# Experts' input by products with a 0/1 slot matrix instead of a gather; routing per tile inside the output projection; residual gates loaded during attention

## The reference

```
x  = x + gt_a * (attention(...) @ w_o)            # context rows too, in layer 0
h  = rmsnorm(x, g_ffn) * (1 + sc_f) + sh_f        # 512 tokens in layer 0, 256 in layer 1
g  = argmax(h @ w_group + b_group)                # 1 of 4 groups
e1, e2 = top 2 of the group's 8 experts by h @ w_router + b_router
y  = sum over the two of wt_e * (silu(h @ w_gate[e]) * (h @ w_up[e])) @ w_down[e]
x  = x + gt_f * y
```

## Time and profile before

| | us |
|---|---|
| median of 3 runs (2517.99 to 2520.10) | 2518.36 |
| profiled execution | 2517.32 |
| its span | 2515.5 |
| PE busy | 2069.2 (82%) |
| DVE busy | 584.7 (23%) |
| ACT busy | 393.8 (16%) |
| L667, all expert products | 750.1, PE idle before them 197.3 |
| DMA `ring<-in_w_up` in the chain | 28% of the span |

### The profile page before, as it was taken

The page is one execution under the profiler, slowest core; times in us unless marked ns, Lnnn a source line. Parts: engine busy times, 40 slices in busy tenths (PEclk is TensorE's granted clock), DMA queues, the critical chain, the costliest instruction groups (busy, mean ns, idle before and its releaser), DMA issues.

```text
span 2515.5 us, 19888 instructions
## 1 busy us (share of the span) xinstructions
PE 2069.2 (82%) x8087; PEld 959.4 (38%) x8087; DVE 584.7 (23%) x1244; ACT 393.8 (16%) x815; POOL 103.7 (4%) x156
## 2 busy tenths in 40 slices
PE   4999986777787776895877877758988899998898
PEld 1444434333332333553333332324435444444543
DVE  1234434100000004743000000011055231035322
ACT  1123400000000002331000000001132211031310
POOL 1000010100000001001000000001000001000000
PEclk9999996889989998996998999988999799998789
DMA  9256552799999997204999999967421134431020
GB/s 351 100 197 229 212 209 100 282 428 426 428 428 427 428 426 287 101 27 162 424 429 427 428 428 428 428 279 262 139 91 42 67 120 154 139 123 67 34 92 25
DMA packets 119726, 621.03 MB, mean 247 GB/s; under 512 B 8016, under 2 KB 10336, under 8 KB 95056
## 3 DMA queue, kind: packets, MB, share of 16 engines
q1 hardware_dynamic: 101664, 561.17, 55.5%
q0 software_dynamic: 13360, 41.74, 4.8%
q10 hardware_dynamic: 4608, 16.78, 1.6%
HBM read 594.43 MB, written 25.23 MB: 246 GB/s over the span
## 4 chain that ended last, share of the span: by engine, by line
PE 58%; DMA 31%; DVE 7%; ACT 2%; issue 1%; SPq 1%; POOL 0%; DVEq 0%; ACTq 0%; POOLq 0%
DMA ring<-in_w_up 28%; PE bank L667 11%; PE bank L874 9%; PE bank L855 7%; PE bank L745 5%; PE bank L1019 3%; PE bank L545 3%; PE bank L801 3%; PE bank L1035 2%; PE bank L631 2%; PE bank L607 1%; PE bank L492 1%; PE bank L857 1%; DMA ring<-in_w_ada 1%; PE bank L816 1%
## 5 line engine op out<-in xcount | busy, mean ns | idle before, releaser
L667 PE MATMUL bank<-ring,big 128*64 128x512 f32 x3072 | 750.1, 645 | 197.3 <-DMA ring<-in_w_gate 99.3
L667 PEld LDWEIGHTS bank<-ring,big 128*64 128x64 f32 x3072 | 263.6, 148 | 660.8 <-issue 620.8
L874 PE MATMUL bank<-ring,big 128*128 128x512 f32 (+1 forms) x512 | 220.3, 594 | 1.7 <-issue 1.7
L855 PE MATMUL bank<-ring,big 128*128 128x512 f32 x384 | 185.1, 638 | 0.0
L1785 DVE TENSOR_TENSOR big<-big,bank 128x512 f32<-128x512 f32 x32 | 22.0, 688 | 668.5 <-PE bank L667 668.5
L874 PEld LDWEIGHTS bank<-ring,big 128*128 128x128 f32 x512 | 98.9, 194 | 122.4 <-issue 122.4
L745 PE MATMUL bank<-ring,big 128*128 128x512 f32 x320 | 140.5, 599 | 0.0
L1053 ACT ACTIVATE big<-bank 128x512 f32<-128x512 f32 (+3 forms) x102 | 57.4, 575 | 444.4 <-PE bank L874 204.7
L855 PEld LDWEIGHTS bank<-ring,big 128*128 128x128 f32 x384 | 76.9, 205 | 99.5 <-issue 99.2
L801 PE MATMUL bank<-ring,big 128*128 128x512 f32 x192 | 85.0, 602 | 6.6 <-DVE big L1760 6.6
L1019 PE MATMUL bank<-ring,big 128*128 128x512 f32 x192 | 85.7, 605 | 4.4 <-ACT big L1053 4.4
(11 more groups left out here) (374 smaller groups left out, 1868.8 us busy)
## 6 DMA issues: line engine op xcount, KB each, us to landing
ring<-in_w_gate SPq DMA_DIRECT2D x64, 2048.0 KB, 18.4
ring<-in_w_up SPq DMA_DIRECT2D x64, 2048.0 KB, 19.6
ring<-in_w_down SPq DMA_DIRECT2D x64, 2048.0 KB, 19.8
ring<-in_w_in SPq DMA_DIRECT2D x26, 2048.0 KB, 7.7
ring<-in_w_ada SPq DMA_DIRECT2D x24, 2048.0 KB, 14.0
y_d<-big ACTq DMA_DIRECT2D x32, 512.0 KB, 10.3
ring<-in_w_qkv SPq DMA_DIRECT2D x6, 2048.0 KB, 19.9
ring<-in_w_branch SPq DMA_DIRECT2D x6, 2048.0 KB, 7.6
```

Source lines behind the costliest of these rows:

```text
L667: ins = nc.tensor.matmul(bank[half * CAP:(half + 1) * CAP, :], lhs[:, k, half * CAP:(half + 1) * CAP], w[:, k * step + c0:k * step + c0 + ...
L855: nc.tensor.matmul(u[:, :], HT2[:, k, tile * P:(tile + 1) * P], w[:, k, :], start=(k == 0), stop=False)
L874: ins = nc.tensor.matmul(u[:, 0:n], HT2[:, k, tile * P:(tile + 1) * P], w[:, k, :], start=(k == 0), stop=(k == KD - 1))
```

## The change

1. `h` stays in SBUF (`H`, all tiles). `turn` makes the transposed input of a pair as a product of h with a 0/1 matrix `OH` (token by slot of this pair): for each of 8 column groups, one matmul per tile, accumulated. `h_d`, the slot map and all gathers into `XE` are gone. VectorE builds `OH` of pair b + 2 during pair b. Overflow blocks do the same in their loop.
2. Router product, choice, positions and slots are done tile by tile inside the output projection, for the tile before; what the first pair does not need (counts, overflow list, final destinations, weights) is `weigh`, behind the first turn.
3. The gates of layer 0 are loaded after the bias of piece 6 is issued, in mid-attention. Pieces from 2 on share one stage buffer, so the bias of piece p + 1 is loaded after piece p is stored; layer 1's shift columns and scale columns are now items behind pieces 6 and 7 each.
4. The window mask of layer 0 is a product of "negid" and "before" in place of a product of the identity and a stored mask.

The diff, cut to its core:

```diff
 # TensorE, attention's fills
-                if in_columns(p) and PIECES[p][1] == 2:
+                if in_columns(p):
                     items += [("column", p, half) for half in range(2)]
 # TensorE, experts
-                def turn(j, gathered):
-                    pe.wait_ge(s_xe[j], gathered)
+                def turn(b, j):
+                    pe.wait_ge(s_oh, b + 1)
                     for k in range(KD):
-                        ins = nc.tensor.transpose(banks[k // 4][:, (k % 4) * P:(k % 4 + 1) * P],
-                                                  XE[j].rearrange("p (n k) -> p k n", k=KD)[:, k, :], ident)
+                        for tile in range(tiles):
+                            ins = nc.tensor.matmul(banks[k // 4][:, (k % 4) * P:(k % 4 + 1) * P],
+                                                   H[:, tile, :].rearrange("p (n k) -> p k n", k=KD)[:, k, :], OH[j][:, tile, :],
+                                                   start=(tile == 0), stop=(tile == tiles - 1))
                     ins.then_inc(s_xt, 1)
 # TensorE, output projection
+                def positions(tile):
+                    u = unit("D")
+                    pe.wait_ge(s_sel, due(s_sel))
+                    if tile:
+                        nc.tensor.matmul(u[:, 0:32], C("ones"), MSC[:, tile, :], start=True, stop=False)
+                    ins = nc.tensor.matmul(u[:, 0:32], C("before"), MS[:, tile, :], start=(tile == 0), stop=True)
+                    ...
                 for tile in range(tiles):
                     pe.wait_ge(s_otaken, GROUPS_BEFORE[layer] + KV * (tile + 1))
-                    (two products with w_o, then norm_turn(tile - 1); routing after the loop)
+                    u = unit("D")
+                    wo_part(u, tile, 0, range(KD)).then_inc(s_unitD, 1)
+                    if tile:
+                        norm_turn(tile - 1, H[:, tile - 1, :])
+                        turned.append((count["A"], count["D"]))
+                        ur = unit("D")
+                    u = unit("D")
+                    wo_part(u, tile, 1, range(KD // 2))
+                    if tile:
+                        router(ur, tile - 1)
+                    wo_part(u, tile, 1, range(KD // 2, KD)).then_inc(s_unitD, 1)
+                    ...
+                    if tile:
+                        positions(tile - 1)
+                norm_turn(tiles - 1, H[:, tiles - 1, :])
+                turned.append((count["A"], count["D"]))
+                router(unit("D"), tiles - 1)
+                positions(tiles - 1)
                 experts(layer)
 # VectorE, slots (route per tile makes LG, OHG, LM, OH1, OH2, MS, MSC of the tile: 17 operations)
+            def slots(layer, tile):
+                u = take()
+                V.tensor_tensor(POS[:, tile, :], u[:, 0:32], C("slot0"), ALU.add)
+                if tile == (LAT if layer == 1 else NT) - 1:
+                    V.tensor_copy(CNT, u[:, 32:64])
+                V.tensor_scalar(FAR[:, tile, :], u[:, 0:32], float(CAP), None, ALU.is_ge).then_inc(s_outD, one(s_outD))
+                dve.wait_ge(s_outD, so_far(s_outD))
+                V.scalar_tensor_tensor(LM[:, tile, :], FAR[:, tile, :], float(2 * NBMAX * P), POS[:, tile, :], ALU.mult, ALU.add)...
+                sums_of(slice(tile, tile + 1), LM[:, tile:tile + 1, :], DST)
+            def slot_rows(tile, j, dest):
+                V.tensor_scalar(OH[j][:, tile, :], C("iota"), dest[:, tile, 0:1], None, ALU.is_equal).then_inc(s_v, one(s_v))
+                dve.wait_ge(s_v, so_far(s_v))
+                return V.scalar_tensor_tensor(OH[j][:, tile, :], C("iota"), dest[:, tile, 1:2], OH[j][:, tile, :], ALU.is_equal, ALU.add)
+            def all_slot_rows(tiles, j, b, s_sh, s_one, s_oh):    # the same two, for every tile of pair b, from DSB
+            def shifted(tiles, b, s_sh):
+                V.tensor_scalar(DSB[:, 0:tiles, :], DST[:, 0:tiles, :], float(P * b), None, ALU.subtract).then_inc(s_sh, 1)
 # VectorE, output projection
                 for tile in range(tiles):
+                    out_part(tile, 0)
+                    if tile:
+                        half_out(tile - 1)
+                        route(layer, tile - 1)
+                    out_part(tile, 1)
+                    ...
+                    modulated(tile)
+                    if tile:
+                        slots(layer, tile - 1)
+                        slot_rows(tile - 1, 0, DST)
                 half_out(tiles - 1)
-                dve.wait_ge(s_hst[0], due(s_hst[0], 16))
-                dve.wait_ge(s_hst[1], due(s_hst[1], 16))
-                route(layer, tiles)
+                route(layer, tiles - 1)
+                slots(layer, tiles - 1)
+                slot_rows(tiles - 1, 0, DST).then_inc(s_oh, 1)
 # VectorE, experts: in each block, behind the copy of the turned rows
+                    if rows_next:
+                        shifted(tiles, b + 2, s_sh)
+                        all_slot_rows(tiles, j, b + 2, s_sh, s_one, s_oh)
+                shifted(tiles, 1, s_sh)
+                all_slot_rows(tiles, 1, 1, s_sh, s_one, s_oh)
                 xt_half(1, 0)
+                weigh(layer, tiles)
 # GpSimd
-            for p in range(STAGES):
-                ada_bias(p)
+            ada_bias(0)
+            ada_bias(1)
             layer_vectors(0)
             for p in range(len(PIECES)):
+                if in_columns(p):
+                    pool.wait_ge(s_mt, 2 if p < 2 else 2 + PIECES[p][1] // 2 + 1)
+                else:
                     ada_store(p)
                     stored += 32
                     pool.wait_ge(s_mod, stored)
-                if p + STAGES < len(PIECES):
-                    ada_bias(p + STAGES)
+                if 1 <= p < len(PIECES) - 1:
+                    ada_bias(p + 1)
+                if p == 5:
+                    pool.wait_ge(s_zeroed, 16)
+                    gates(0, 2)
             for layer in range(2):
-                gates(layer, 2)
+                if last:
+                    gates(layer, 2)
                 pool.wait_ge(s_otaken, GROUPS_AFTER[layer])
                 modulation(layer, "g_ffn", 3, tiles // LAT)
-                (stores of h, waits for the slot map, all gathers into XE)
                 gates(layer, 5)
```

More of the change, by code:

```diff
@@ L794, in _, with wo_part, router @@
                 w1, n1 = weights(("wo", layer, 1))
+                wo = [w.rearrange("p (k n) -> p k n", k=KD) for w in (w0, w1)]
+                def wo_part(u, tile, c, ks):
+                    for k in ks:
+                        ins = nc.tensor.matmul(u[:, :], hT(tile, k), wo[c][:, k, :], start=(k == 0), stop=(k == KD - 1))
+                    return ins
+                def router(u, tile):
+                    pe.wait_ge(s_outA, turned[tile][0])
+                    pe.wait_ge(s_outD, turned[tile][1])
+                    for k in range(KD):
+                        ins = nc.tensor.matmul(u[:, 0:36], hT(tile, k), WRT[:, k, :], start=(k == 0), stop=(k == KD - 1))
+                    ins.then_inc(s_unitD, 1)
@@ L1398, in modulated_half, with modulated @@
                 ins.then_inc(s_outD, one(s_outD))
-            def modulated(tile, store):
+            def modulated(tile):
                 dve.wait_ge(s_ss, due(s_ss))
@@ new lines, in slots @@
+            def slots(layer, tile):
+                u = take()
+                V.tensor_tensor(POS[:, tile, :], u[:, 0:32], C("slot0"), ALU.add)
[3 more added lines that the diff above has]
+                dve.wait_ge(s_outD, so_far(s_outD))
+                V.scalar_tensor_tensor(LM[:, tile, :], FAR[:, tile, :], float(2 * NBMAX * P), POS[:, tile, :], ALU.mult, ALU.add).then_inc(s_v, one(s_v))
@@ new lines, in all_slot_rows, with weigh @@
+                dve.wait_ge(s_one, b)
+                for tile in range(tiles):
+                    ins = V.scalar_tensor_tensor(OH[j][:, tile, :], C("iota"), DSB[:, tile, 1:2], OH[j][:, tile, :], ALU.is_equal, ALU.add)
+                ins.then_inc(s_oh, 1)
+            def shifted(tiles, b, s_sh):
+                V.tensor_scalar(DSB[:, 0:tiles, :], DST[:, 0:tiles, :], float(P * b), None, ALU.subtract).then_inc(s_sh, 1)
+            def weigh(layer, tiles):
+                T = slice(0, tiles)
+                gm, km, m1, m2, a, b4 = (x[:, T] for x in tm)
+                V.tensor_tensor(EG[:, T, 0:4], LG[:, T, 0:4], bc(gm.unsqueeze(2), P, tiles, 4), ALU.subtract)
+                V.tensor_tensor(EG[:, T, 4:5], m2.unsqueeze(2), m1.unsqueeze(2), ALU.subtract).then_inc(s_gx, one(s_gx))
@@ L1754, in _ @@
                 scales(tiles // LAT)
-                for tile in range(tiles):
-                    gate = GATE[tile // LAT]
-                    for c in range(2):
-                        cs = slice(c * 512, (c + 1) * 512)
-                        u = take()
-                        V.tensor_tensor(RES, u[:, :], gate[:, cs], ALU.mult).then_inc(s_outD, one(s_outD))
-                        dve.wait_ge(s_outD, so_far(s_outD))
```

(13 more changed lines are left out.)

340 lines of the change are left out of this document (118 added, 222 removed).

## The result

The changed kernel takes 2578.56 us (median of 4 runs, 2574.08 to 2580.23), the kernel before beside it 2518.18 (4 runs, 2517.74 to 2520.10): ratio 1.0235, 95% interval [1.0218, 1.0253]. It is slower by 60 us, where 60 us less was forecast; the time lies outside the range. Rival A's mechanism happened, at a higher price than it had been given.

The account below looks back on a forecast made before the run. Expert stages were taken as bound by weight bytes, 20% of PE free. Layer 0: 13.5 + 13.4 + 1.8 - 0.9 = 27.8; layer 1: 16.5 + 14.2 + 1.8 = 32.5; 60.3 off 2517.3 gives 2457.0, median 2458, range 2440 to 2482.

Parts of the forecast that it names:

- Rival A: Layer 0's turn doesn't stream: 0.217 us per instruction, PE's period 36.0, slower at 2540 us; chance 0.09.
- Part 2: Turn products replacing the gather: 0.12 us per instruction, 7.7 us in layer 0, 3.8 in layer 1; 3 us charged.
- 15 such periods: Each layer's expert stage has 15 periods of 31.86 us behind its first pair, each 1.1 us shorter without the gather.
- Part 1: No gather in the expert stages: period 31.86 to 30.7 us per pair, 16.5 us gained in each layer.
- Rival C: The gather's bytes did not hold the weights: both expert stages keep 31.86 us, total 2488; chance 0.07.
- Part 3: Routing inside the output projection: gate product 13.4 us earlier in layer 0, 14.2 in layer 1, plus 1.8 each.
- Rival D: Output projection stretches, tile handoffs cost 3 us more, gate loads late: half of 27.6 goes, about 2472; chance 0.10.
- Rival B: PE sets layer 0's stage mildly: 0.14 to 0.17 us per instruction, period 31 to 33, about 2472; chance 0.14.
- Part 4: Gates loaded early, in attention: two loads fewer save 2.5 us, against bias and column costs; sum -0.9 us.
- The late bias: With one stage buffer for ada pieces, bias p + 1 follows store p: 0.4 us late at the last piece.
- The rule that was weighed: Skill's weight load price, 107 ns per 128 columns: end to end 0.214 us per turn instruction, period 35.8; overlapped 0.107.

Follow-up runs that it names:

- e6: e3 with rows laid out in neighbouring pairs (turn weights 2 columns apart) and only VectorE's addition permuting: 2464.51 us, ratio 0.9791 to the kernel before.
- e3: e2 with layer 0's modulation loads issued ahead of the last ada store: 2474.24 us, ratio 0.9827 to the kernel before.
- b1: The kernel before, with the gather of pairs 2 to 15 replaced by a load of 4 bytes a partition: 2484.46 us, ratio 0.9867.
- e2: e1 with a second staging buffer for the ada pieces again: 2476.22 us, ratio 0.9837 to the kernel before.
- e1: The changed kernel with VectorE permuting rows so the turn's 128 weight columns are neighbours: 2476.51 us, ratio 0.9845 to the kernel before.

## Why the prediction was wrong, step by step

**Part 2 failed, and it alone turned the sign.** The step: "The strided weights are not more: L659's strided transposes are 8 in 1.15 us. I take 0.12". Measured 0.241 (15.45 / 64), twice that and outside the bounds of 0.107 to 0.217 as well. The argument had two halves, each true: a real product with neighbouring columns streams at 0.12 (L890), a strided transpose too (L659). The row for both together did not exist, and I let a transpose stand for a product. The upper bound failed for a different reason: it was a contiguous form at half clock, so it bounded the clock and not the access pattern. PE's period came out at 20.82 + 15.45 + 1.16 = 37.43 where 29.8 was worked out; 15 periods cost 15 x (37.43 - 30.7) = 101 us, the first turns 6.7 and 2.7 more (15.52 and 7.90 us against 8.8 and 5.2). e6, with a turn of 7.75 us, measures 2464.5, 6 us off the forecast (it also has e3's order of loads, whose 2 us are within scatter).

The whole error, 2574.1 against 2457.0 in the profiled executions, is 117 us. By the stretches of the table 103 lie in layer 0's experts (88 lost where 15.3 were to be gained), 10 ahead of its first gate product, 1.5 in layer 1 and 2.3 in the rest. A smaller slip is in "15 such periods": the first of them was about 26 us before, and 14 were 31.86 ((934.96 - 488.91) / 14).

**Rival A** had the place and the mechanism of a turn that does not stream right, and the price too low: 2540 from 0.217, against 2578.6. With the measured turn its own sum gives 2458 + 13.5 + 84 + 9 = 2565; part 4, the first pair and scatter are most of what is left. Its deciding point, 0.20 us an instruction, was passed by 0.241, but no run lies near it. Its reason for was the one that held ("no row has this form"); at 0.09 I valued it as a doubt and not as an unmeasured cost in a stage with 1 us of margin.

**Part 1** was right: 30.40 to 30.67 us a pair in layer 1, 30.6 in b1 and 34 us there against the 33 of two stages. Rival C is excluded by both.

**Part 3** was right. From layer 0's first output part (359.69) to the gate product (452.70) are 93.0 us, forecast 86.0, and the turn has 6.7 of the 7.0 difference; the tiles come 17.9 us apart (17 to 18 forecast). Layer 1: 1202.26 to 1253.53, 51.3 us against 48.2, with 2.7 of the turn. Rival D is excluded. Rival B is too: the period is 37.43 and not 31 to 33.

**Part 4** had the wrong sign, by 5 us: the first output part is 4.0 us later (359.69 against 355.68), not 0.9 earlier. Chain of the changed kernel:

```profile
330.33 5.15 DMA big<-in_b_ada
...
337.88 6.72 DMA mod_d<-big
...
344.89 2.11 POOL big L2084 x4
347.00 10.19 DMA big<-mod_d
```

The modulation loads are issued at 344.89 instead of 337.70, 7.2 us later; with two fewer of them they land 12.3 us behind their issue instead of 15.5, a gain of 3.2 (forecast 2.5). The late bias, which I charged at 0.4, is not the reason (e2). The attention is the larger part: from its first `ada` product to its last score product at L564 (L532 to L564; in the kernel before L545 to L579) it takes 155.3 us in the kernel before (150.0 to 305.3) and 155.2 in b1, and 159.4 in each of the changed kernel, e1, e2 and e3. These 4.1 us belong to the change, where 3.4 were charged, but not for the reason given. PE's waits for VectorE in this stretch are 9.9 us in sum against 8.9: the new ones at the column items, 1.7 and 1.3, take the place of one of the waits at the row adds. The other 3.2 us are busy time of PE (149.9 against 146.8), with a lower granted clock (0.83 from 240 to 260 us, before 1.00) whose share was not isolated. Another 1.9 us of the later issue lie ahead of the attention and vary between executions of the same work (the first such product at 150.3 us in e1, 152.9 in e3), so about 2 of the 5 us are scatter between executions. The last 1.2 lie between the attention's end and the issue, and no run says why.

**The rule that was weighed, and one that was not.** With neighbouring columns an instruction takes 0.115 us, so load and product overlap. The Trainium skill, "TensorE: Matmul & The Clock Gate", section "LDWEIGHTS (loading the stationary operand)", prices a load by its columns, 107 ns for 128; of the two estimates made from it, 0.214 end to end and 0.107 overlapped, the trace is near the second. It was not what decided. What decided is in these rows: 0.121 us with two weight columns in each 16 bytes, 0.233 with one. The Trainium skill, "SBUF — State Buffer", section "Door 1: The DMA port swizzle", in a note on cachelines, says that SBUF has lines of 16 bytes and that a pattern needs at least two hits in a line to run at full rate; by this rule, with which the trace agrees (0.121 and 0.233), a stride of 8 float32 would have been a term with a price. It also says that 4 float32 can be strided for free; here 4 apart is slow (0.233), and the measurement decides.

## What to carry to other kernels

When an instruction takes an operand in a new access pattern, the pattern is part of its price: look for a row with the same operation and the same innermost stride, and where there is none, take the double as an end of the range. A transpose's row does not price a product. And where a stage has 1 us of slack in 31, an unmeasured term of 64 instructions decides the sign, so it is the one to measure alone before the change is judged.

## What the runs showed of the hardware

- An instruction of a float32 product (two make one product) with 128 weight columns takes 0.115 us where they lie side by side, 0.121 where they are 2 apart, 0.177 at 3, 0.233 at 4, 0.240 at 8 and 9 and 0.219 at 16; 64 columns 8 apart take 0.127 (6.1 / 48). Moving columns pay about the same (0.229 at 4, 0.238 at 8), and both sides at once no more (0.242). Transposes do not pay (0.117 at 8); no run says why.
- In these stretches the strided load does not follow TensorE's clock. The changed kernel's first turn, part of it at half clock, takes as long as a later one (15.52 and 15.45 us); e1's, with neighbouring columns, takes 10.06 against 7.41 (the changed kernel, then e1):

```profile
436.37 15.52 PE bank L646 x64
```

```profile
439.32 10.06 PE bank L646 x64
```

  In the first of them PE does 11 instructions in 2.6 us at a granted clock of 0.50 and 14 in 3.0 at 1.00, 0.24 and 0.21 as whole instructions are counted; the contiguous turn of e1 does 12 in 2.6 us at 0.50 and 29 in 3.0 at 1.00. Windows of either, the changed kernel first (its rows leave out the column of POOL; after the busy times come the granted clock, the DMA share and GB/s):

```profile
436.40:439.00 2.60, 2.60 (x11) 2.60 (x12) 0.00 (x0) 0.00 (x0) 0.50 0.00 0
442.00:445.00 3.00, 3.00 (x14) 3.00 (x14) 0.00 (x0) 0.00 (x0) 1.00 0.00 0
```

```profile
439.40:442.00 2.60, 2.60 (x12) 2.60 (x13) 1.90 (x8) 0.00 (x0) 0.00 (x0) 0.50 0.00 0
445.00:448.00 3.00, 3.00 (x29) 3.00 (x29) 0.00 (x0) 0.00 (x0) 0.00 (x0) 1.00 0.00 0
```

- VectorE takes about 1.6 times as long with a strided float32 side (2.06 us for 1.28, 1.98 for 1.21), once, however many sides are strided, and no longer where elements come in neighbouring pairs (1.22). ScalarE's copy takes 2.04 us for 1.04 with strided reads; its pairs were not measured.
- Expert weights move at 428 GB/s in runs of 16 KB, and at 401 with two thirds of the bytes in runs of 2 KB, with the DMA engines full in both.
